# Input projections of a four-branch mixer as three-pass products, and eight output-gate tiles projected in the gate stage

## The reference

```
cs = silu(c);  sh1, sc1, gt1, sh2, sc2, gt2 = split(cs @ ada_w + ada_b)
h    = rms(x, norm1_w) * (1 + sc1) + sh1
proj = h @ w_in        # q,k,v and gates of four branches, then 4 x 1024 merge gates
out_a = rms(gated_delta(conv(...)))  * silu(g_z)      # chain g
out_b = rms(hgrn2(...))              * silu(h_g)      # chain h
out_c = rms((ssd(conv(...)) + d*x)   * silu(s_z))     # chain s
out_d = rms(mlstm(...))              * sigmoid(m_o)   # chain m
merged = sum_n sigmoid(gate_n) * (out_n @ w_branch_n)
x = x + gt1 * (merged @ w_out)
x = x + gt2 * ((silu(h2 @ A) * (h2 @ B)) @ ffn_w_out)   # h2 from norm2
```

## Time and profile before

| | |
|---|---|
| median of 3 runs | 1296.57 us (1296.25 to 1301.6) |
| profiled execution | 1298.08 us, its span 1296.3 us |
| TensorE busy | 1209.0 us (93%) |
| VectorE busy | 549.6 us (42%) |
| ScalarE busy | 360.9 us (28%) |
| DMA | 116.70 MB, mean 90 GB/s |

### The profile page before, as it was taken

How to read it: one execution, slowest core, us unless ns; L and a number is a source line. 1 busy time by engine, 2 the same in 40 slices (tenths; PEclk the granted TensorE clock), 3 DMA queues, 4 the chain that set the end, 5 groups by cost and what they waited for, 6 DMA issues and landing times. The chain is left out here.

```text
span 1296.3 us, 26018 instructions
## 1 busy us (share of the span) xinstructions
PE 1209.0 (93%) x11325; PEld 1082.5 (84%) x11325; DVE 549.6 (42%) x1116; ACT 360.9 (28%) x529; POOL 11.6 (1%) x29
## 2 busy tenths in 40 slices
PE   5599989989999999889999999969999999989997
PEld 3378767757777776889999998959999999989996
DVE  1351764566566744453333335462222222353322
ACT  2332371272212111552222221142222222341111
POOL 0000110000000000000000000000000000000000
PEclk9799999999998987989999999979999999989998
DMA  9812732023333031555333321312332332223201
GB/s 310 248 35 75 123 100 96 22 83 99 99 99 100 6 95 34 125 77 169 85 90 92 92 89 44 98 33 66 97 97 66 97 97 56 75 81 90 71 20 70
DMA packets 191030, 116.70 MB, mean 90 GB/s; under 512 B 36650, under 2 KB 189351, under 8 KB 190678
## 3 DMA queue, kind: packets, MB, share of 16 engines
q1 hardware_dynamic: 190358, 115.16, 32.2%
q0 software_dynamic: 576, 0.14, 0.1%
HBM read 108.31 MB, written 6.96 MB: 89 GB/s over the span
## 5 line engine op out<-in xcount | busy, mean ns | idle before, releaser
L746 PE MATMUL ps<-scr_parts 128*128 128x272 f32 x2688 | 521.7, 293 | 16.3 <-DVE hT_parts L2414 8.5
L746 PEld LDWEIGHTS ps<-scr_parts 128*128 128x128 f32 x2688 | 429.6, 191 | 20.3 <-issue 13.6
L746 PE MATMUL ps<-hT_parts,scr_parts 128*128 128x272 f32 x1408 | 391.3, 291 | 0.0
L746 PEld LDWEIGHTS ps<-hT_parts,scr_parts 128*128 128x128 f32 x1408 | 262.0, 190 | 0.0
L2316 DVE TENSOR_TENSOR scr_parts<-ring,scr_parts 128x1024 fp32r<-128x1024 f32 (+1 forms) x100 | 128.9, 1289 | 306.4 <-ACT scr_parts L1580 303.7
L746 PE MATMUL ps<-hT,ring 128*128 128x272 f32 x960 | 247.9, 410 | 3.0 <-ACT pj L1451 3.0
L1580 ACT ACTIVATE scr_parts<-ring 128x1024 fp32r<-128x1024 f32 (+1 forms) x100 | 111.0, 1111 | 490.1 <-PE ps L746 489.3
L746 PEld LDWEIGHTS ps<-hT,ring 128*128 128x128 f32 x960 | 182.5, 196 | 44.5 <-issue 3.9
L746 PE MATMUL ps<-pj_parts,scr_parts 128*128 128x272 f32 x992 | 168.8, 295 | 5.7 <-DVEq L1707 5.7
L746 PEld LDWEIGHTS ps<-pj_parts,scr_parts 128*128 128x128 f32 x992 | 142.8, 192 | 7.3 <-DVEq L1707 6.3
L746 PE MATMUL ps<-scr 64*64 64x64 f32 (+6 forms) x2336 | 86.0, 234 | 12.9 <-DVEq L1707 5.1
(11 more groups left out here) (307 smaller groups left out, 941.0 us busy)
## 6 DMA issues: line engine op xcount, KB each, us to landing
ring<-in_w_in_dram SPq DMA_DIRECT2D x62, 512.0 KB, 6.7
ring<-in_ada_w_dram SPq DMA_DIRECT2D x48, 512.0 KB, 6.6
ring<-in_ffn_w_in_dram SPq DMA_DIRECT2D x44, 512.0 KB, 5.0
ring<-in_ffn_w_out_dram SPq DMA_DIRECT2D x16, 384.0 KB, 3.6
ring<-in_ffn_w_out_dram SPq DMA_DIRECT2D x16, 320.0 KB, 4.2
ring<-in_w_out_dram SPq DMA_DIRECT2D x8, 512.0 KB, 5.4
x_scratch<-scr SPq DMA_DIRECT2D x1, 2176.0 KB, 13.4
Q<-x_scratch SPq DMA_DIRECT2D x1, 2176.0 KB, 10.9
```

The costliest lines, as they stand in the source:

```text
L746: return pe.matmul(out, lhsT, rhs, start=start, stop=stop, skip_group_check=True)
```

## The change

The input projections become three-pass products. In the norm, ScalarE now writes the high part of the normalised input, `x_hi`, in the eight `pj` tiles of the output gates (Z_TILES), which are free until then, and VectorE the low part over `hT` (`h_lo`). For each of the 22 remaining feature tiles the weights are split in two halves of four contractions: ScalarE writes the high part in one of two small buffers (`wx_hi`, `weights_high`), and VectorE the low part over the ring slot itself (`weights_low`). A high part waits until TensorE has read that buffer for the last time. A tile is one unit of four parts (contraction half by column half), and its two column halves are evicted separately (`read_group`). The small projection `s_w` is split likewise (`s_whi`, `s_wlo`). The planner gets these as new steps.

The four groups of output gates leave the window. They are loaded behind it (`Z_ORDER`) and are products 0 to 7 of the gate stage; ScalarE evicts the first two with Silu and the rest raw, and activates these after the eighth. `h_hi` is copied from `x_hi`; no low part is made there any more. The merge gates are all evicted with Sigmoid at once. LAG becomes 4, counted from product 8, so the first lift comes after 12 products where it came after 7.

```diff
-MIX_ORDER = [0, 1, 2, 9, 10, 4, 5, 6, 11, 12, 13, 3, 8, 7, 14]
+MIX_ORDER = [0, 1, 2, 9, 10, 4, 5, 6, 11, 12, 13]
+Z_ORDER = [8, 3, 7, 14]
...
 GBUF = [10, 11, 24, 25, 20, 21]
-N_RAW = 6
-LAG = 7
+Z_TILES = [2 * g + c for g in Z_ORDER for c in range(2)]
+LAG = 4
 PIECE = KF // 2 * P
-M_WOUT = 4 * KD
+M_GATE = len(Z_TILES)
+M_WOUT = M_GATE + 4 * KD
 M_FFA = M_WOUT + KD
 M_FFB = M_FFA + 2 * KF
...
-for _n in range(len(MIX_ORDER)):
-    SEQUENCE += [("mix", 4 * _n + _v) for _v in range(4)]
-    if _n >= ADA_FROM:
-        SEQUENCE[-1:] = [("ada", _n - ADA_FROM), SEQUENCE[-1], ("turn", _n - ADA_FROM)] if _n - ADA_FROM < 8 else SEQUENCE[-1:]
+for _n in range(2 * len(MIX_ORDER)):
+    SEQUENCE.append(("mix", _n))
+    if _n >= 8 and _n % 2 == 1:
+        SEQUENCE.append(("ada", _n // 2 - 4))
+    if _n >= 10 and _n % 2 == 0:
+        SEQUENCE.append(("turn", _n // 2 - 5))
+SEQUENCE += [("turn", 6), ("ada", 7), ("turn", 7)]
 UNITS = len(SEQUENCE)
-POS = {u: n for n, u in enumerate(SEQUENCE)}
...
     if t == PRE:
-        s = [("w", "pe"), ("rz", "dve"), ("rb", "act"), ("ri", "dve"), ("rexp", "act"), ("rv", "dve")]
+        s = [("whi", "act"), ("wlo", "dve"), ("w", "pe"), ("rz", "dve"), ("rb", "act"), ("ri", "dve"), ("rexp", "act"), ("rv", "dve")]
```

```diff
+            def three(out, wh, wl, hi, lo, start, stop):
+                mm(out, wh, hi, start, False)
+                mm(out, wl, hi, False, False)
+                return mm(out, wh, lo, False, stop)
             def unit_part(u, part_):
-                if part_ == 0 and u >= 2:
-                    pe.wait_ge(x_read, u - 1)
                 kind, v = SEQUENCE[u]
+                bank = part_ % 2 if kind == "mix" else 0 if kind == "ada" else 1
+                if (part_ < 2 if kind == "mix" else part_ == 0) and BANK_FREE[(u, bank)]:
+                    pe.wait_ge(x_read, BANK_FREE[(u, bank)])
                 if kind == "mix":
-                    n, c, h = load_of[("mixer", v // 4)], v // 2 % 2, v % 2
-                    if part_ == 0:
-                        landed(pe, n % R, n)
-                    for k in range(4 * part_, 4 * part_ + 4):
-                        if u == 0:
-                            pe.wait_ge(stream_in, k + 1)
-                        at = k * 256 + c * P
-                        last = mm(ps[:, u % 2, 0:HN], ring[:, n % R, at:at + P], hT[:, k, h * HN:(h + 1) * HN], k == 0, k == KD - 1)
+                    e, h = part_ // 2, part_ % 2
+                    if h == 0:
+                        pe.wait_ge(x_split, 2 * v + e + 1)
+                    wh, (_, wl) = mix_hi(e), mix_weights(v, e)
+                    for k in range(4 * e, 4 * e + 4):
+                        if v == 0 and h == 0:
+                            pe.wait_ge(h_split, k + 2)
+                        c = slice(h * HN, (h + 1) * HN)
...
-                pre.after(pe, 0, "norm1")
                 rest.begin(pe, PRE, "s_w")
-                pe.wait_ge(d_wsm, 80)
+                pe.wait_ge(h_split, KD + 1)
                 for h in range(2):
+                    c = slice(h * HN, (h + 1) * HN)
                     for k in range(KD):
-                        last = mm(ps[:, 2 + h, 0:HN], wsm[:, k, :], hT[:, k, h * HN:(h + 1) * HN], k == 0, k == KD - 1)
+                        last = three(ps[:, 2 + h, 0:HN], wsm_hi[:, k, :], wsm_lo[:, k, :], x_hi[k][:, c], h_lo[:, k, c], k == 0, k == KD - 1)
                 last.then_inc(rest_s, 1)
...
-            for k in range(4 * KD + LAG):
-                if k < 4 * KD:
+            for k in range(M_WOUT + LAG):
+                if k < M_WOUT:
                     if k >= 2:
                         pe.wait_ge(gate_read, k - 1)
-                    product(k, 2 * (k % 2), *h_parts, tiles_split=0 if k == 0 else None, tiles=gate_in)
-                if 1 <= k < 5:
-                    n = k - 1
+                    product(k, 2 * (k % 2), *h_parts, tiles_split=0 if k == 0 else None, tiles=gate_in_hi)
+                if 2 <= k < 6:
+                    n = k - 2
```

```diff
+            def weights_high(i, e):
+                raw, _ = mix_weights(i, e)
+                n = load_of[("mixer", i // 2)]
+                landed(act, n % R, n)
+                if i and e == 0:
+                    act.wait_ge(x_half, i)
+                elif i:
+                    act.wait_ge(x_done, TILE_DONE[i - 1])
+                act.activation(mix_hi(e), raw, ACT.Copy).then_inc(x_split_hi, 1)
+            for e in range(2):
+                weights_high(0, e)
             pre.begin(act, 0, "norm1")
+            act.wait_ge(normed, 1)
+            for n in range(KD // 2):
+                act.activation(x_hi_samples(n), hT[:, 2 * n:2 * n + 2, T:TA], ACT.Copy)
+            act.drain().then_inc(h_split_hi, 1)
             for k in range(KD):
-                act.wait_ge(normed, k + 1)
-                act.activation(hT[:, k, 0:T], hT[:, k, 0:T], ACT.Identity, bias=mod[:, k, 0:1]).then_inc(stream_in, 1)
+                act.wait_ge(normed, k + 2)
+                act.activation(x_hi[k][:, 0:T], hT[:, k, 0:T], ACT.Identity, bias=mod[:, k, 0:1]).then_inc(h_split_hi, 1)
             act.drain().then_inc(pre_s, 1)
...
+                act.wait_ge(d_wsm, 80)
+                act.activation(wsm_hi, wsm, ACT.Copy).then_inc(rest_s, 1)
+                yield
...
                     for k in range(KD):
-                        act.activation(h_hi[:, k, :], hT[:, k, :], ACT.Copy).then_inc(gate_in_hi, 1)
+                        act.activation(h_hi[:, k, :], x_hi[k].bitcast(F32), ACT.Copy).then_inc(gate_in_hi, 1)
...
+            def z_out(m, func):
+                act.wait_ge(w_done, m + 1)
+                act.activation(two(pj[:, Z_TILES[m], :]), ps[:, 2 * (m % 2):2 * (m % 2) + 2, 0:HN], func).then_inc(gate_read, 1)
...
+            for m in range(2):
+                high(m + 2)
+                z_out(m, ACT.Silu)
+            for m in range(2, M_GATE):
+                n = m - 2
+                high(m + 2)
+                z_out(m, ACT.Copy)
+                if n < 4:
+                    mid.begin(act, 0, f"o_rs{n}")
+                    for f in range(2):
+                        act.activation(two(rms[n][f]), ps[:, 4 + 2 * f:6 + 2 * f, 0:HN], ACT.Ln,
+                                       scale=1.0 / (P if n == 2 else DK), bias=colp[:, 3:4])
+                    act.drain().then_inc(mid_s, 1)
+                    for f in range(2):
+                        act.activation(rms[n][f], rms[n][f], ACT.Exp, scale=-0.5)
+                    act.drain().then_inc(rms_ready, 1)
             act.drain()
-            for k in range(N_RAW):
-                act.activation(gates[k], gates[k], ACT.Sigmoid).then_inc(gate_ready, 1)
...
+            for z in (GZ, GZ + 1, HG, HG + 1):
+                act.activation(pj[:, z, :], pj[:, z, :], ACT.Silu).then_inc(z_ready, 1)
+            for z in (MO, MO + 1):
+                act.activation(pj[:, z, :], pj[:, z, :], ACT.Sigmoid).then_inc(z_ready, 1)
+            for k in range(4 * KD):
+                if k == len(GBUF):
+                    act.wait_ge(branch_ready, 1)
+                high(M_GATE + k + 2)
+                gate_out(k)
+                if k >= LAG + 4 and (k - LAG) % 4 == 0 and k < 4 * KD - 3:
+                    merged_high((k - LAG) // 4 - 1)
```

```diff
+            def weights_low(i, e):
+                raw, lo = mix_weights(i, e)
+                dve.wait_ge(x_split_hi, 2 * i + e + 1)
+                dve.tensor_tensor(lo, raw, mix_hi(e).bitcast(F32), SUB).then_inc(x_split, 1)
             coefficients(V_N1, 0)
             normalise_samples(xT0, 0)
+            dve.drain().then_inc(normed, 1)
+            normalise(xT0, 0)
+            dve.wait_ge(h_split_hi, 1)
+            for n in range(KD // 2):
+                r = dve.tensor_tensor(h_lo[:, 2 * n:2 * n + 2, T:TA], hT[:, 2 * n:2 * n + 2, T:TA], x_hi_samples(n).bitcast(F32), SUB)
+            r.then_inc(h_split, 1)
             for k in range(KD):
-                normalise(xT0, k)
+                if k + 1 < KD:
+                    normalise(xT0, k + 1)
+                dve.wait_ge(h_split_hi, k + 2)
+                dve.scalar_tensor_tensor(out=h_lo[:, k, 0:T], in0=hT[:, k, 0:T], scalar=mod[:, k, 0:1],
...
+            for m in range(3):
+                low(m)
...
-                if k + 8 < M_WOUT + 2:
-                    low(k + 8)
+                if M_GATE + k + LAG + 1 < M_WOUT + 2:
+                    low(M_GATE + k + LAG + 1)
```

232 lines of the change are left out of this document (136 added, 96 removed).

## The result

| | before | changed |
|---|---|---|
| median (range), runs | 1296.41 (1295.72 to 1301.6), 4 | 1329.10 (1328.01 to 1329.29), 4 |
| ratio (95% interval) | | 1.0242 (1.0214 to 1.0269) |
| profiled span, us | 1296.3 | 1325.8 |
| mean granted clock of TensorE | 0.961 | 0.929 |

The change costs 2.4%. I had said 1299 (1270 to 1322), so the time lies outside my range.

A forecast was written before the change was run, and what follows sets the result against it. TensorE, busy in 93% of the span, was taken as the bound, VectorE in the emptied last tiles. The terms 10.5 + 0 - 1.5 - 38.3 - 8.9 + 48.0 - 7.8 = +2.0 on 1296.57 gave 1299 us (1270 to 1322).

The forecast's parts named there:

- Steps 1, 3 and 5: To the convolutions' tail transposes +10.5 us; tiles up to tile 2's second level step -1.5; handover to gate stage -8.9.
- Step 1: Start to the convolutions' tail transposes: +10.5 us (+6 to +15), TensorE idle for 14 behind VectorE's row stage.
- One sign: TensorE idle for 10 us or more just before the row stage's end, at about 90 to 102 us.
- Step 2: Convolutions, 125.5 to 187.4 us: 0 (-3 to +5), twelve low splits fitting in VectorE's time without work.
- Step 4: Rest of the tiles, without projections, 340.5 to 513.8 us: 135 us, so -38.3, with 40% of VectorE's waits staying.
- A sign: In the last 130 to 140 us of the tiles, VectorE busy over 75% and TensorE under 75%.
- C: Rival: half clock on TensorE through the last tiles, 152 us there for 135, total 1316; chance 0.20.
- D: Rival: splits late through convolutions and tiles, 20 of 44 by 0.9 us, +18, total 1317; chance 0.10.
- B: Rival: the three chains pack well without projections, last tiles 118 us, total 1277; chance 0.30.
- Step 6: Gate stage: +48.0 us for eight added products, -7.8 for an idle time and half clock that go.
- The 4.4 us idle time: TensorE's idle time of 4.41 us at 574.94 in the gate stage, forecast to go with the half clock around it, -7.8.

The follow-up runs named there:

- e3: The changed kernel with VectorE's 14.3 us row stage cut into five stages: 1318.5 us, ratio 1.0144.
- e4: The changed kernel with plain fp32 products and no weight splits in the window, so the move of the eight output-gate tiles alone: 1322.5 us, ratio 1.0180.
- e1: The changed kernel with 400 useless matmuls put into TensorE's idle time behind the last unit of the second modulation: 1332.2 us, ratio 1.0243.
- e6: The changed kernel with 28 extra VectorE additions of 384 columns behind the second chain's levels in tiles 2 to 4: 1344.6 us, ratio 1.0335.
- e15: The changed kernel without two VectorE operations in each level of the second chain in tiles 2 to 4: 1325.7 us, ratio 1.0199.
- e16: The changed kernel with 196 useless matmuls in TensorE's planned gaps of the tail: 1322.1 us, ratio 1.0172.
- e13: The changed kernel with 30 extra VectorE additions of 384 columns behind the first chain's steps in tiles 2 to 4: 1344.9 us, ratio 1.0358.
- e14: The changed kernel with 25 extra VectorE additions behind the third chain's steps in tiles 1 to 4: 1340.3 us, ratio 1.0306.
- e2: The changed kernel with the eight output-gate tiles projected a second time in the window, results dropped: 1336.4 us, ratio 1.0286.
- e10: Three-pass products without the move: all 30 tiles in the window, gate stage as before, output-gate results dropped: 1295.6 us, ratio 0.9962.

## Why the prediction was wrong, step by step

**Steps 1, 3 and 5 held**, to 0.4, 1.8 and 0.3 us. Step 1 is shown by e3: cutting the stage gives back 8.6 of the 10.9 us. One sign was off in size: the idle time ahead of the late split was 8.2 us and not 10 or more. The small projection ended when I had said, at 80.5, but the first half of tile 1 waited for an eviction until 88.08 and then ran at the lower clock to 93.9. The sum came out because it hung on the split at 101.3.

**Step 2, 0 predicted, +5.0.** I let twelve splits fit into VectorE's 18.7 us without work. In the trace its time outside waits, between these landmarks, grew from 46.2 us to 55.4 (9.2), and its waits shrank from 16.6 to 12.4 only. e4, without splits, has 64.1 us here, 1.3 more than before. The mistake is of the same kind as the next.

**Step 4 is the step that failed, 18 us.** "I take 40% of these waits to stay": 72% stayed, 39.3 of 54.4. VectorE's work was right to about 1 us. I had read waits on TensorE as waits on its queue, which empties when projections go. Most of them stay when it has emptied: they are waits for the step that was just given to TensorE, and the path through the tail changes between the engines. A sign was missed with it: VectorE was busy for 67% of the tail (102.7 of 153.0 us), not over 75%. The range of waits over all runs but the kernel before is narrow, 32.1 to 45.9, whether TensorE has 110 us to do in the tail or 154 (e1), and whether VectorE has 102.7 us busy, 118 (e6) or 96 (e15). Of the 18 us, the clock holds at least 6.8 (e16). It may hold nearly all: the 40.4 us of TensorE on the path from 438.8 on, at the two durations of the earlier trace rows (1.97 and 1.15 us), would be 16.8 us shorter at the full clock, an estimate that takes the path to stay as it is. How the other 11 us are shared between the clock and dependent steps is open; no run had the tail at full clock without extra work in it. Nor was another order of the chains' stages tried.

**The rivals.** C gave 152 us for step 4, and it took 153.0, but the sum behind it was wrong: TensorE was not the bound with 151 us of work, it was busy for 110, and only the part from 438.8 ran at 0.50. That its 152 was met is luck. Its cause is real and worth 7 us at least. The rule I had cited from the Trainium skill (TensorE: Matmul & The Clock Gate, Part 1: The HAM clock gate) is that "the default state is throttled, and activity releases the throttle". The traces agree: in e16 more activity took the clock from 0.71 to 0.86, and in e6, e13 and e14 the same TensorE work, spread over a longer tail, ran at 0.65 to 0.66. D was taken for 20 late splits all through; TensorE waited for the ring's splits three times, 11.6 us, 8.2 of them in step 1, and in the convolutions 3.5. B falls.

**Step 6, +40.2 predicted, +42.9.** The 4.4 us idle time went as said. What I left out is the clock that the gate stage inherits: its first 5.4 us, 511.9 to 517.3, are at 0.50, which is 2.7 us. But before, its first 3.5 us were at 0.51, which was 1.7:
```profile
525.10:528.60 3.50, 3.44 (x15) 3.47 (x16) 3.50 (x6) 3.49 (x7) 0.00 (x0) 0.51 1.22 289
```
So the clock explains 1.0 of the 2.7 us over the forecast, and the rest is open.

**In all**, 43 us of TensorE's work were saved and 48 of cover moved out of a stretch in which cover costs almost nothing (e2: 3.4 us of tail for it) into one where it costs its whole length (42.9). Before the change the tail carried 83.4 us of matmuls on the ring for 173.3 - 153.0 = 20 us of time. That is the exchange that made it slower, and e4 shows it without the three-pass products. e10, with them and without the move, is 0.4% faster than before.

## What to carry to other kernels

Before work is moved off a full engine, ask whether the waits of the others on it are waits on its queue or on the step just handed over; e2 and the gap-filled run (e16) told this here, each by one run: add useless work to the full engine and see how little it costs. Work that lay between the steps of dependent chains was nearly free here, so it should only move to a place where it is free too. Ask too what clock the emptied stretch will get: here the work that was moved out had also held the clock up. A long stage on an in-order engine (14.3 us here) should be cut where another engine's inputs pass through the same queue.

## What the runs showed of the hardware

- Useless matmuls made a kernel faster: 196 of them in TensorE's gaps took the granted clock in the tail from 0.71 to 0.86 and 7 us off the time (ratio 1.0242 to 1.0172).
- The lower clock outlasted the stretch that brought it: the dense gate stage ran at 0.50 for its first 5.4 us.
- GpSimd's subtraction of 128x512 took 1375 ns where VectorE's took 692. With 14 of them in that stretch, VectorE's operations of the convolutions took 54.9 us where 43.6 stood before; those of 128x32 took 449 ns in the mean for 245.
- 28 additions of 384 columns on VectorE were paid in full (15.6 us busy, tail 17.9 longer) in a stretch in which VectorE waited for 39.3 us.
